# Waits between the first gathers of activations in the PEER stage of a hybrid decoder step

## The reference

```python
def block(hb):
    ...                       # product-key retrieval: 8 heads, top 16 of 16384 experts
    a = jax.nn.gelu(jnp.einsum('td,ted->te', hb, u[e]), approximate=False)
    return jnp.einsum('te,ted->td', (g * a).astype(hb.dtype), v[e])
```

## Time and profile before

| | us |
|---|---|
| median of 3 runs | 1870.18 |
| lowest, highest | 1859.30, 1872.53 |
| profiled execution, its own time | 1854.62 |
| its span, first to last instruction | 1852.5 |
| TensorE busy | 1798.2 (97%) |
| VectorE busy | 1218.8 (66%) |
| GpSimd busy | 487.2 (26%) |

### The profile page before, as it was taken

The page is one execution under the profiler, slowest core; times in us unless marked ns, Lnnn a source line. Parts: engine busy times, 40 slices in busy tenths (PEclk is TensorE's granted clock), DMA queues, the critical chain, the costliest instruction groups (busy, mean ns, idle before and its releaser), DMA issues.

```text
span 1852.5 us, 31068 instructions
## 1 busy us (share of the span) xinstructions
PE 1798.2 (97%) x12753; PEld 1324.2 (71%) x12753; DVE 1218.8 (66%) x2611; ACT 572.1 (31%) x984; POOL 487.2 (26%) x515
## 2 busy tenths in 40 slices
PE   8999999989999999999999999999969999999999
PEld 6743445768888888888888888888736666566665
DVE  7558677555998983755556333444248788888885
ACT  1002134310234223444334333343213333333331
POOL 0000100000355650000000000000268778777640
PEclk9999999899999999999999999999979999999999
DMA  4422622002122333465555755555568999999991
GB/s 166 107 88 109 202 92 92 1 4 114 47 92 92 138 138 138 184 229 206 198 205 191 278 184 178 200 192 192 204 231 330 366 384 379 371 376 378 376 387 47
DMA packets 116238, 365.11 MB, mean 197 GB/s; under 512 B 12041, under 2 KB 72697, under 8 KB 104321
## 3 DMA queue, kind: packets, MB, share of 16 engines
q1 hardware_dynamic: 90416, 288.02, 41.6%
q0 software_dynamic: 25680, 75.10, 11.3%
HBM read 299.78 MB, written 63.31 MB: 196 GB/s over the span
## 4 chain that ended last, share of the span: by engine, by line
PE 87%; DVE 10%; issue 2%; ACT 1%; DMA 0%; SPq 0%; DVEq 0%; ACTq 0%
PE psum L2012 34%; PE psum L2066 27%; PE psum L1718 22%; PE psum L2033 2%; DVE u_lo L1457 1%; PE psum L1846 1%; PE psum L1724 1%; DVE rest L1384 0%; PE psum L1766 0%; PE psum L1809 0%; DVE ixs L1401 0%; DVE CI L1430 0%; DVE CI L1422 0%; DMA xT<-in_xT 0%; DVE crest L1419 0%
## 5 line engine op out<-in xcount | busy, mean ns | idle before, releaser
L2066 PE MATMUL psum<-w_hl,v_hi 128*128 128x384 bf16 x1920 | 468.0, 326 | 0.0
L2012 PE MATMUL psum<-h_hi,u_hi 128*128 128x260 bf16 x2048 | 395.1, 274 | 3.2 <-DVE u_lo L1457 2.5
L2012 PE MATMUL psum<-h_lo,u_hi 128*128 128x260 bf16 x2048 | 395.0, 274 | 0.0
L2012 PE MATMUL psum<-h_hi,u_lo 128*128 128x260 bf16 x2048 | 394.9, 274 | 0.0
L706 POOL DMA_INDIRECT trow<-in_v,t_lists x136 | 171.6, 1262 | 664.2 <-ACT act_f L916 588.1
L2066 PE MATMUL psum<-w_hl,v_lo 128*128 128x384 bf16 x960 | 313.0, 326 | 0.0
L1457 DVE TENSOR_TENSOR u_lo<-u_raw,u_hi 128x1024 bf16<-128x1024 f32 x128 | 153.9, 1217 | 209.3 <-ACT u_hi L904 209.2
L2066 PEld LDWEIGHTS psum<-w_hl,v_hi 128*128 128x128 bf16 x1920 | 187.9, 98 | 123.3 <-issue 0.2
L916 ACT ACTIVATE act_f<-psum 128x520 f32<-128x520 f32 x128 | 77.4, 605 | 465.4 <-PE psum L2012 465.4
L2012 PEld LDWEIGHTS psum<-h_hi,u_lo 128*128 128x128 bf16 x2048 | 198.7, 97 | 31.3
L2012 PEld LDWEIGHTS psum<-h_lo,u_hi 128*128 128x128 bf16 x2048 | 198.6, 97 | 31.4
(11 more groups left out here) (377 smaller groups left out, 1895.8 us busy)
## 6 DMA issues: line engine op xcount, KB each, us to landing
u_raw<-in_uT SPq DMA_DIRECT2D x32, 2048.0 KB, 9.4
v_raw<-in_v SPq DMA_DIRECT2D x32, 2048.0 KB
wr<-in_w SPq DMA_DIRECT2D x13, 2048.0 KB, 7.6
d_gate<-stage SPq DMA_DIRECT2D x12, 2048.0 KB, 8.1
d_act<-act_f SPq DMA_DIRECT2D x20, 768.0 KB, 4.5
g_in<-d_gate SPq DMA_DIRECT2D x10, 1536.0 KB
a_in<-d_act SPq DMA_DIRECT2D x20, 768.0 KB
g_up<-d_gate SPq DMA_DIRECT2D x12, 768.0 KB, 10.0
```

Source lines behind the costliest of these rows:

```text
L2012: mm = pe.matmul(upair[n % 2][:, f, 0:HALF], w[g % 2][:, k, c * P:(c + 1) * P], hs[:, k, halves[f]], start=(k == 0 and x == 0), stop=(k == ...
L2066: mm = pe.matmul(ybank[m][:, 0:DENSE], w[g % 2][:, c, m * P:(m + 1) * P], w_now[:, z, c, :], start=(g == 0 and c == 0 and x == 0), stop=(g ...
```

## The change

Dots 1 to 15 each wait on GpSimd for the landing of the dot before. Row 4 now follows dot 1, row 5 dot 2, and so on to row 9 behind dot 6. Dots 8 to 15 stood ahead of row 10; now they come two by two behind rows 10 to 13, and from row 14 on two dots follow a row until the old distance is reached at row 18.

```diff
+ALONE = 2 * BATCH
...
                 if s % BATCH == 0 and b >= 2:
                     pool.wait_ge(t_weighed, b - 1)
+                if s >= 1 and s < ALONE:
+                    before = (s - 1) // BATCH
+                    pool.wait_ge(t_dots_in[before % 2], 16 * (BATCH * (before // 2) + (s - 1) % BATCH + 1))
                 pool.indirect_dma_start(t_dots[:, s:s + 1], None, d_acts, bass.IndirectOffsetOnAxis(
...
-            for s in range(BATCH):
+            slot_dot(0)
+            pool.wait_ge(w_prod, NEARLY)
+            for s in range(1, BATCH):
                 slot_dot(s)
-            pool.wait_ge(w_prod, NEARLY)
-            for s in range(4, TROWS):
-                slot_row(s)
-            for s in range(BATCH, 2 * BATCH):
-                slot_dot(s)
+                if s + 3 < TROWS:
+                    slot_row(s + 3)
+            dots = BATCH
             for s in range(TROWS, TSLOTS):
                 slot_row(s)
-                if s + 2 * BATCH - TROWS < TSLOTS:
-                    slot_dot(s + 2 * BATCH - TROWS)
+                for _ in range(2):
+                    if dots < min(TSLOTS, s + 2 * BATCH - TROWS + 1):
+                        slot_dot(dots)
+                        dots += 1
```

## The result

The changed kernel took 1882.02 us (median of 11 runs, 1871.91 to 1889.45), the kernel before 1868.75 us (11 runs, 1858.12 to 1873.75) beside it: 1.0079 times as long, with a 95% interval of 1.005 to 1.0109. It is slower, by about 1%. The forecast was 1866 us, a little less than the kernel before, so the sign is wrong, though the time lies in the range of 1848 to 1888. The profiled execution is 1882.02 us with a span of 1880.0, against 1854.62 and 1852.5; the trace of the kernel before is of an execution shorter than any of the 11.

What follows compares the result with a forecast made beforehand. TensorE was taken as the bound, with a stall in step 1: 20.4 us gained, 18.8 spent on VectorE's wait for dots, net 1.6 less. From the 1870.2 median, 1.6 and 2.6 off gave 1866 us, range 1848 to 1888.

Steps and rivals of the forecast that it cites:

- The bunches go: TensorE's stall in step 1 comes from dots in flight together; without bunches step 1 takes 15.6 us, gain 20.4 us.
- What is late next is VectorE: In-order VectorE, waiting for dots, holds up steps 3 and 4; of 20.4 us, 18.8 are spent again on that wait.
- the mean round trip c: Mean time of the 15 dots' round trips on GpSimd's queue; c = 3.1 us gives -1.6 us.
- the prediction's own formula: Change in time = 15c - 48.2 us, c being the 15 dots' mean round trip; zero at c = 3.2.
- Alone 2.7 us: A dot's round trip on GpSimd's queue with nothing beside it: 2.7 us.
- Beside one stream 3.8 us: A dot's round trip on GpSimd's queue beside a 2 MB stream of v: 3.8 us.
- Behind a row beside a stream 5.2 us: A dot's round trip behind a row that shares with a stream of v: 5.2 us, also the upper end.
- Dots 8 to 15 "behind rows 10 to 13": The second eight round trips begin only when the first eight ended and VectorE has begun: 3.5 us, then 24.1 us.
- Later waits at nothing: New TensorE waits after step 4, for v, gates or rows, were priced at nothing.
- 2.6 us off for the spread: Of the 15.6 us between profile and median, 2.6 us were taken off because the stall's length may vary.
- B: Chain of waits on a loaded queue ahead of step 4: mean trip 4 us, +11.8, so 1882 us; chance 0.17.
- Rival C: Single dots disturb TensorE and ScalarE too, so step 4 starts at 1414.3, +4.7: 1875 us; chance 0.11.

Runs made afterwards that it cites:

- before_again: The kernel before, run again without an edit on another chip, with a trace: 1835.57 us, 1.0001 times the kernel before beside it.

## Why the prediction was wrong

**The bunches go: gain 20.4 us.** In the trace it came as written: steps 1 and 2 are 15.6 us, and ScalarE's cast for step 2 is no longer 36.61 us late. But the reason that was given, "the stall as an effect of dots in bunches", does not hold in general. On four other chips, by their traces, the same bunches leave TensorE alone, and on a fifth the time says so. In the trace of the change on the first chip, the same pattern stands in a place where dots and rows alternate:

```profile
1658.95 0.34 PE L2072 MATMUL psum<-w_hl,v_lo 128*128 128x384 bf16 x1 [0.40 <-issue]
1659.67 0.34 PE L2072 MATMUL psum<-w_hl,v_hi 128*128 128x384 bf16 x1 [0.39 <-issue]
1660.41 0.32 PE L2072 MATMUL psum<-w_hl,v_hi 128*128 128x384 bf16 x1 [0.40 <-issue]
1661.12 0.34 PE L2072 MATMUL psum<-w_hl,v_lo 128*128 128x384 bf16 x1 [0.38 <-issue]
1661.85 0.50 PE L2072 MATMUL psum<-w_hl,v_hi 128*128 128x384 bf16 x2 [0.39 <-issue]
```

One matmul per 0.72 us in place of 0.16, with gaps that no instruction ends, as in the earlier trace rows, for 3 us. No trace on another chip has them. A disturbance of that chip which needs no bunch is one reading; it is argued, not shown, since no later run fell on a chip where the kernel before takes 1868 us. That it fell beside the bunch by mere chance is not borne out by the times: over 11 executions of each kernel the first chip costs the kernel before 33 us against the chip of before_again (1868.75 and 1835.94) and the changed one 10 us (1882.02 and 1872.06), so the change lost 13 us there and not 36. The 23 us between may be a stall that the change prevented, or a disturbance that disappears in TensorE's new waits for VectorE; no run tells which, and what it is stays open.

**What is late next is VectorE.** Right, in order and place: it waits for dots 0 to 7 and for dots 8 to 15, TensorE idles ahead of steps 3 and 4, and the order of VectorE's work carries the one to the other. The sizes were short: 15.0 us of idle time ahead of step 3 where the sum had 2.4, and 18.7 ahead of step 4 where some 14 were expected.

**The step that failed: the mean round trip c.** The sum took 3.1 us for 15 trips; it was 4.26. By the prediction's own formula, 15 x 4.26 - 48.2 = +15.7. Dot 0 was down, by dot 1's issue, 15.1 us after the first gather and not 12.5, 2.6 us more; VectorE took 13.6 us from dot 15 to step 4 and not 15.7, 2.1 us less; and the restart at the lower clock cost 2.4 us (step 4 took 18.0 and not 15.6, at a granted clock of 0.50 until 1430 and 0.93 behind it) and not 1.2. That makes +17.4, and the end of step 4 moved by 17.4. On the chip of before_again, with c at 4.42 and no 20.4 us to win, the formula is 15c - 27.8 and gives +38.5, and the end of step 4 moved by 36.9. Term by term:

- Alone 2.7 us: measured 2.62.
- Beside one stream 3.8 us: dot 1 took 4.3.
- Behind a row beside a stream 5.2 us, called the upper end: dot 2 took 7.1, dot 10 7.5 (1390.63 to 1398.08), dots 4 and 5 6.0 and 6.5. The row behind the 5.2 us could not show this: from 1341 to 1345 no row lay on GpSimd's queue (rows 0 to 3 were done, row 4 was issued at 1343.78), so it priced small packets beside v, and not a row of 0.52 MB ahead of a dot.
- How many are loaded. The sum charged three of 15. Four took about 6.0 us or more (2, 4, 5, 10), dot 11 took 4.9, and dots 1, 8 and 9 between 3.5 and 4.3, the last of them by GpSimd's slow issues and not by a landing. Left out were the loads of activations and gates that SyncE issues at the end of step 1, which the gain itself moves forward, to 1361, right into the chain. A faster step 1 starts these transfers among the waits.

Dots 8 to 15 "behind rows 10 to 13" were priced as a chain that starts 3.5 us after the first; that was right (1379.31 to 1382.79).

**Later waits at nothing.** Right on the chip of before_again (427.5 and 427.8 us). On the first chip the end of the kernel took 7.0 us more, of which the trace shows 4.0 us in waits for VectorE and 2.0 in the gaps above.

**2.6 us off for the spread.** No run bears it out: the stall stands in full in the shortest execution of the kernel before (1854.62 us), so it is not what put the median 15.6 us above the profile. What did stays open. It belongs to that chip, where both kernels take longer than on the others.

**The rivals.** B, a chain of waits on a loaded queue, priced at 1882 us for a mean of 4 us, is what happened; it had a chance of 0.17, on the ground that streams fill only part of the stretch. Rival C left out its own restart of 1.2 us, so it stood at 1876 and not at 1875; that changes nothing. By the figure of the Trainium skill (DMA: Bandwidth & Descriptors, "Anatomy of one DMA", some 2.0 us for such a transfer) the formula gives an estimated gain of 18 us. The trace differs. A gather of 4-byte elements on an idle queue took 2.62 us from issue to issue, 0.6 more; the other 1.6 us of the mean of 4.26 came with what else was on the queues and, for dot 9, with GpSimd's own issues.

## What to carry to other kernels

A wait for a landing costs the trip on the queue as it is loaded at that moment, not the idle trip: here 2.6 us alone and 6 to 7.5 us behind one 0.5 MB gather and beside a load of 2 MB or more. Before putting such waits in a chain, list every transfer that will be in flight beside each of them, with the ones that the hoped-for gain moves forward, and ask which in-order engine stands behind the last one. And a stall that one trace shows once, with no releaser, is to be looked for in a second execution, best on a second chip, before anything is built on its removal.

## What the runs showed of the hardware

- The kernel before took 1868.75 us on the first chip and 1833.6 to 1839.2 us on five others, 1.6 to 1.9% apart, with a granted clock of 0.987 in the first chip's trace and 0.989 to 0.993 in the other four. On the first, two traces have stretches in which TensorE takes one matmul per 0.7 us or more with nothing that releases it: 22 us long in the kernel before, where ScalarE stood still as well, and 3 us long in the changed one.
- After 15.0 and 18.7 us of idle time TensorE restarted at the lower of its two clock levels (granted clock 0.50 from 1412 to 1430): at 1391.82 and 1427.62 two matmuls took 0.82 and 0.80 us that take 0.49 at full clock. After 0.85 us of idle time in before_again they took 0.49.
- Beside a load of v (122 packets, 2.00 MB) GpSimd's queue moved 0.24 MB in 7 us; beside the loads of gates and activations (1665 packets, 2.33 MB) it moved 1.20 MB in 11 us.
- GpSimd took 0.95 us to issue an indirect DMA in most rows, and 1.7 to 2.0 us for those from 1386 to 1392 in the changed kernel, while VectorE was busy.
